# Two squared-ReLU MLPs in a fused fp32 block: wide up products, down products with tokens on partitions, two modulation groups moved

## The reference, cut to what matters

```python
mod = (sc @ w_mod[l] + b_mod[l])[:, None, :]          # 1024 x 6144 for each l
sh1, sc1, g1, sh2, sc2, g2 = jnp.split(mod, N_MOD, axis=-1)
...
u = rms_norm_2(h, norm2_g[l]) * (1.0 + sc2) + sh2     # modulate
a = jnp.maximum(u @ w_mlp1[l], 0.0)                   # 1024 -> 4096
h = h + g2 * ((a * a) @ w_mlp2[l])                    # 4096 -> 1024
```

## Time and profile before

| | |
|---|---|
| median of 3 runs | 1496.66 us (1496.38 to 1497.01) |
| the profiled execution | 1496.03 us, its span from first to last instruction 1494.2 us |
| granted TensorE clock | 1.0 over the span |
| busy: TensorE / VectorE / ScalarE / GpSimd | 98% / 82% / 55% / 8% |
| `mlp0`, from TensorE's first down to the pool stage | 1124.33 to 1290.82 us |
| `mlp1`, the same to TensorE's last matmul | 1323.24 to 1490 us |

### The profile page before, as it was taken

One profiled execution on the slowest core, in us unless ns is written; L12 is line 12 of the kernel. 1 busy time (PEld: TensorE's weight loads), 2 busy tenths in 40 slices (PEclk: granted clock), 3 DMA queues, 4 the chain that ended last, 5 costly groups with the idle time before them and its releaser, 6 DMA issues.

```text
span 1494.2 us, 26569 instructions
## 1 busy us (share of the span) xinstructions
PE 1471.7 (98%) x10462; PEld 1368.6 (92%) x10462; DVE 1226.4 (82%) x1722; ACT 820.8 (55%) x1195; POOL 116.4 (8%) x70
## 2 busy tenths in 40 slices
PE   7999999999999999999999999999999999999999
PEld 7999999999998899999779999987689999999998
DVE  7999898989988879999777988884777998885564
ACT  6554568655456645556765455554654544564442
POOL 0013100001311102111000211100001212000000
PEclk9999999999999999999999999999999999999999
DMA  7667663556675547666243776743235887346540
GB/s 271 252 242 254 239 234 130 225 187 238 238 267 197 227 168 282 236 246 250 85 141 136 287 257 250 253 156 137 106 142 203 305 289 274 141 165 222 177 170 29
DMA packets 44419, 310.43 MB, mean 208 GB/s; under 512 B 5728, under 2 KB 5984, under 8 KB 7200
## 3 DMA queue, kind: packets, MB, share of 16 engines
q1 hardware_dynamic: 42048, 303.33, 55.3%
q0 software_dynamic: 1696, 4.68, 1.1%
q10 hardware_dynamic: 576, 1.05, 0.2%
HBM read 307.93 MB, written 1.05 MB: 207 GB/s over the span
## 4 chain that ended last, share of the span: by engine, by line
PE 94%; DVE 3%; ACT 2%; issue 0%; DMA 0%; SPq 0%; DVEq 0%; ACTq 0%
PE psum L1901 18%; PE psum L1981 18%; PE psum L1907 17%; PE psum L1908 17%; PE psum L1992 9%; PE psum L2148 3%; PE psum L2154 3%; PE psum L2153 3%; DVE w_lo L1074 1%; PE psum L2466 1%; PE psum L2477 1%; PE psum L2396 0%; PE psum L2361 0%; DMA x<-x_in 0%; PE psum L2267 0%
## 5 line engine op out<-in xcount | busy, mean ns | idle before, releaser
L1074 DVE TENSOR_TENSOR w_lo<-raw,w_hi 128x1024 fp32r<-128x1024 f32 x478 | 591.0, 1252 | 78.0 <-ACT w_hi L528 77.4
L528 ACT ACTIVATE w_hi<-raw 128x1024 fp32r<-128x1024 f32 x478 | 486.1, 1047 | 66.3 <-PE psum L1901 40.4
L1901 PE MATMUL psum<-hid_hi,w_hi 128*128 128x256 f32 x1220 | 346.1, 284 | 1.1 <-DVE hid_lo L1352 1.1
L1907 PE MATMUL psum<-hid_lo,w_hi 128*128 128x256 f32 x1220 | 345.3, 283 | 0.0
L1908 PE MATMUL psum<-hid_hi,w_lo 128*128 128x256 f32 x1220 | 345.2, 283 | 0.0
L1901 PE MATMUL psum<-u,w_hi 128*128 128x256 f32 (+1 forms) x1104 | 317.3, 287 | 11.0 <-DVE u L1171 9.7
L1907 PE MATMUL psum<-u,w_hi 128*128 128x256 f32 (+1 forms) x1104 | 311.4, 282 | 0.0
L1908 PE MATMUL psum<-u,w_lo 128*128 128x256 f32 (+1 forms) x1104 | 310.9, 282 | 0.0
L1981 PE MATMUL psum<-u,w_hi 128*128 128x512 f32 x1152 | 274.8, 391 | 0.0
L1981 PEld LDWEIGHTS psum<-u,w_hi 128*128 128x128 f32 x1152 | 211.7, 188 | 41.0
L1901 PEld LDWEIGHTS psum<-hid_hi,w_hi 128*128 128x128 f32 x1220 | 233.9, 192 | 1.6 <-DVE hid_lo L1352 1.5
(11 more groups left out here) (272 smaller groups left out, 1411.3 us busy)
## 6 DMA issues: line engine op xcount, KB each, us to landing
raw<-stream SPq DMA_DIRECT2D x288, 1024.0 KB, 4.8
buf<-tab POOLq DMA_DIRECT2D x2, 768.0 KB, 5.5
x<-x_in SPq DMA_DIRECT2D x2, 512.0 KB, 7.0
buf<-ctx_in POOLq DMA_DIRECT2D x1, 1024.0 KB, 8.1
buf<-poolmat POOLq DMA_DIRECT2D x1, 1024.0 KB, 5.1
out<-x ACTq DMA_DIRECT2D x4, 256.0 KB, 2.1
buf<-late POOLq DMA_DIRECT2D x1, 640.0 KB, 4.1
mod<-mod_row POOLq DMA_DIRECT2D x28, 2.0 KB, 1.9
```

The lines of the kernel that those rows point to most:

```text
L528: sc.activation(w_hi[:, u], raw[:, u], ACT.Copy).then_inc(S.hi_ready, 1)
L1074: ve.tensor_tensor(w_lo[:, u], raw[:, u], w_hi[:, u].bitcast(F32), ALU.subtract).then_inc(S.lo_ready, 1)
L1901: ins = te.matmul(dst, w_hi[:, w], hi, start=first, stop=False, skip_group_check=True)
L1907: te.matmul(dst, w_hi[:, w], lo, start=False, stop=False, skip_group_check=True)
```

## The change

- **Ups from step 5 on** (`WIDE = 5`). VectorE makes x · gain · rstd into a spare buffer (`both_full`, 8 chunks of 256 columns), ScalarE adds the shift and rounds (`both_hi`, 8), VectorE makes the rest (`both_lo`, 8). TensorE then makes each up unit of steps 5 to 15 as 8 matmuls of 512 columns and 8 of 256. ScalarE copies the low half out of PSUM (`copy_sums`), VectorE adds the halves (`added`) and takes ReLU and square in one instruction. The shift column, the scaling and the ReLU on ScalarE go in those steps.
- **Downs 0 to 13 with tokens on partitions** (`down_tokens`): `hid` is now the stationary operand (128 x 128) and 512 columns of weights the moving one, so a unit is 12 matmuls of 512 columns in place of 24 of 256. At the end the four banks are split into hi and lo (`token_sums_hi` on ScalarE, `token_sums_lo` on VectorE, four each, during up 15). Down 14 is made in the old layout into the cleared banks, then 32 matmuls with the identity as moving operand, 128 columns each, turn the split sums round and add them (`turn_sums`), then down 15.
- **Early steps reordered.** The scaling of step 1 has a buffer of its own and comes right behind that of step 0. The `both_*` work is put between steps 1 and 3 on ScalarE and VectorE, and the pumps of this part are placed anew.
- **Modulation.** Groups 22 and 23 move from `mlp0` to `mlp1`. In `mlp0` the units per step are now 2, 1, 1 repeated over steps 3 to 14; in `mlp1` one in each of steps 4 to 11.
- `u`'s rows are 1032 columns apart (1024 before), and the MLPs' narrow operands lie at their end; in the pool stage `shift_operand(1)` on ScalarE comes behind the first block of operands.

The core of the diff, in the order constants, ScalarE, VectorE, TensorE:

```diff
-HOME = {"ffn0": range(0, 4), "ffn1": range(4, 8), "ffn2": range(8, 13), "ffn3": range(13, 18), "mlp0": range(18, 24),
-        "mlp1": range(24, 24)}
+HOME = {"ffn0": range(0, 4), "ffn1": range(4, 8), "ffn2": range(8, 13), "ffn3": range(13, 18), "mlp0": range(18, 22),
+        "mlp1": range(22, 24)}
...
-           "ffn3": [0] * 4 + [1, 1, 2, 1, 2, 1] + [1] * 12, "mlp0": [0] * 3 + [2] * 12 + [0], "mlp1": [0] * MLS}
+           "ffn3": [0] * 4 + [1, 1, 2, 1, 2, 1] + [1] * 12, "mlp0": [0] * 3 + [2, 1, 1] * 4 + [0], "mlp1": [0] * 4 + [1] * 8 + [0] * 4}
...
+WIDE = 5
+TOKENS = MLS - 2
...
+                def both_hi(k):
+                    act.wait_ge(S.both_full, NC * m + k + 1)
+                    sc.activation(m_both[:, k, 0:T], ck(buf[3])[:, k, :], ACT.Identity, bias=part(m, 3, k)).then_inc(S.both_hi, 1)
...
+                relu(0)
+                relu(1)
+                hi(0)
+                pump_to(c0 + RING - 1)
+                relu(2)
+                hi(1)
+                pump_to(c0 + 9)
+                for k in range(4):
+                    both_hi(k)
+                hi(2)
+                pump_to(c0 + 3 + RING)
+                for k in range(4, NC):
+                    both_hi(k)
+                pump_to(pumped(2))
+                for j in range(3, MLS):
+                    (relu if j < WIDE else copy_sums)(j)
+                    if j < MLS - 2:
+                        pump_one(pumped(j))
+                    hi(j)
+                    if j == MLS - 2:
+                        for b in range(4):
+                            token_sums_hi(b)
+                    pump_to(pumped(j))
...
+                scaled(0, t2, "s", 4)
+                scaled(1, t_one, "s_one", 6)
+                squared(0)
+                pump_to(c0 + AHEAD)
+                low(0)
+                scaled(2, third, "s_third", 2)
+                pump_to(c0 + RING - 1)
+                squared(1)
+                pump_to(c0 + RING)
+                low(1)
+                pump_to(c0 + 9)
+                for k in range(4):
+                    both_full(k)
+                squared(2)
+                pump_to(c0 + 2 + RING)
+                low(2)
+                pump_to(c0 + 3 + RING)
+                for k in range(4, NC):
+                    both_full(k)
+                for k in range(4):
+                    both_lo(k)
+                pump_to(pumped(2))
+                for j in range(3, MLS):
+                    if j < WIDE:
+                        scaled(j, t2, "s", 4 + 2 * (j % 2))
+                    else:
+                        added(j)
...
+                    low(j)
+                    if j == 3:
+                        for k in range(4, NC):
+                            both_lo(k)
+                    if j == MLS - 2:
+                        for b in range(4):
+                            token_sums_lo(b)
+                    pump_to(pumped(j))
...
+                    if j >= WIDE:
+                        if j == WIDE:
+                            pe.wait_ge(S.both_lo, NC * (m + 1))
+                        wide_hi(c, 0, bank, m_both).then_inc(S.unit_used, 1)
+                        wide_hi(c + 1, 0, bank + 1, m_both)
+                        wide_lo(c, 0, bank, 0, m_both)
+                        began, done = wide_lo(c + 1, 0, bank + 1, 0, m_both)
+                        began.then_inc(S.unit_used, 1)
+                        done.then_inc(S.up_ready, 1)
+                        begun[0] = c + 1
...
+                def token_products(c, n, par, b, first, last, begins):
+                    tt, w = b // 2, slice((c % RING) * UNIT + (b % 2) * 512, (c % RING) * UNIT + (b % 2 + 1) * 512)
+                    t = slice(n * T + tt * P, n * T + (tt + 1) * P)
+                    ins = te.matmul(psum[:, b, :], hid_hi[:, par, t], w_hi[:, w], start=first, stop=False, skip_group_check=True)
+                    if begins:
+                        ins.then_inc(S.unit_used, 1)
+                    te.matmul(psum[:, b, :], hid_lo[:, par, t], w_hi[:, w], start=False, stop=False, skip_group_check=True)
+                    return te.matmul(psum[:, b, :], hid_hi[:, par, t], w_lo[:, w], start=False, stop=last, skip_group_check=True)
+
...
+                def turn_sums():
+
+                    pe.wait_ge(S.ident_ready, 1)
+                    for half in (sum_hi, sum_lo):
+                        for n in range(NC):
+                            for tt in range(2):
+                                te.matmul(bank2(n // 2)[:, n % 2, tt * P:(tt + 1) * P],
+                                          half[:, 2 * tt + n // 4, (n % 4) * P:(n % 4 + 1) * P], ident_r[:, :], start=False, stop=False,
+                                          skip_group_check=True)
 
...
-                down(0, first=True)
-                down(1)
-                for j in range(3, MLS):
+                down_tokens(0)
+                down_tokens(1)
+                for j in range(3, MLS - 1):
                     up_pair(j)
-                    down(j - 1)
+                    down_tokens(j - 1)
+                up_pair(MLS - 1)
+                down(TOKENS, first=True)
+                turn_sums()
                 down(MLS - 1, last=True)
 
```

More of the change, by code:

```diff
@@ L200, in __init__ @@
         self.up_copied = sem("up_copied")
+        self.both_full = sem("both_full")
+        self.both_hi = sem("both_hi")
+        self.both_lo = sem("both_lo")
+        self.ident_ready = sem("ident_ready")
+        self.tok_sums = sem("tok_sums")
+        self.sums_hi = sem("sums_hi")
+        self.sums_lo = sem("sums_lo")
         self.up_added = sem("up_added")
@@ L509, in _ @@
                     sum_squares(n)
+            sum_groups("mlp1")
         @block.scalar
@@ new lines, in low, with both_full, both_lo @@
+                def low(j):
+                    dve.wait_ge(S.hid_hi_ready, h0 + j + 1)
+                    ve.tensor_tensor(hid_lo[:, j % 2, :], h32, hid_hif[:, j % 2, :], ALU.subtract).then_inc(S.hid_ready, 1)
+                v = ck(buf[3])
+                def both_full(k):
+                    ve.scalar_tensor_tensor(v[:, k, :], x[:, k, :], ty(gain, k), rstd[:, :], ALU.mult, ALU.mult).then_inc(S.both_full, 1)
+                def both_lo(k):
+                    dve.wait_ge(S.both_hi, NC * m + k + 1)
+                    ve.scalar_tensor_tensor(m_both[:, k, T:2 * T], v[:, k, :], part(m, 3, k), m_bothf[:, k, 0:T], ALU.add, ALU.subtract)\
+                      .then_inc(S.both_lo, 1)
@@ L1790, in _ @@
             sqrelu("mlp0")
-            modulation_in(HOME["mlp0"][3])
+            modulation_in(HOME["mlp0"][-1])
             add_bias(1, 24, 40)
@@ L1855, in _ @@
             sqrelu("mlp1")
-            modulation_in(HOME["mlp0"][-1])
+            modulation_in(HOME["mlp1"][-1])
             add_bias(1, 40, 48)
@@ L1980, in wide_hi @@
                 for k in range(NC):
-                    ins = te.matmul(bank2(bank), w_hi[:, at + k * P:at + (k + 1) * P], u_both[:, k, :], start=k == 0, stop=False,
+                    ins = te.matmul(bank2(bank), w_hi[:, at + k * P:at + (k + 1) * P], both[:, k, :], start=k == 0, stop=False,
                                     skip_group_check=True)
@@ L1991, in wide_lo @@
                 for k in range(NC):
-                    ins = te.matmul(bank2(bank)[:, 1, :], w_lo[:, at + k * P:at + (k + 1) * P], u_hi[:, k, 0:T], start=False,
+                    ins = te.matmul(bank2(bank)[:, at_half, :], w_lo[:, at + k * P:at + (k + 1) * P], hi[:, k, 0:T], start=False,
                                     stop=k == NC - 1, skip_group_check=True)
@@ new lines, in down_tokens @@
+                def down_tokens(j):
+                    c, par = unit_at(name, "down", j), j % 2
+                    pe.wait_ge(S.hid_ready, h0 + j + 1)
+                    if j < TOKENS - 1:
+                        for n in range(2):
+                            unit_ready(c + n)
+                            for b in range(4):
+                                if j == 0 and n == 0:
+                                    third_read(b)
+                                ins = token_products(c + n, n, par, b, j == 0 and n == 0, False, b == 0)
+                        if j == 0:
+                            ins.then_inc(S.first_down, 1)
+                    else:
+                        unit_ready(c + 1)
+                        for b in range(4):
+                            token_products(c, 0, par, b, False, False, b == 0)
+                            token_products(c + 1, 1, par, b, False, True, b == 3).then_inc(S.tok_sums, 1)
+                    begun[0] = c + 1
```

132 lines of the change are left out of this document (71 added, 61 removed).

## The result

The kernel after takes **1514.92 us** (median of 4 runs, 1513.73 to 1516.48), the kernel before in turn with it 1496.52 us (1496.09 to 1497.01): a ratio of 1.0124 with the interval 1.0112 to 1.0136, slower by 18.4 us. The forecast was 1500.4 us with a range to 1506.5. The direction was right; the size was wrong by more than four times, and the time lies outside the range.

The account below looks back on a forecast made before the run. TensorE, busy 98%, was taken as the bound, VectorE second. On 1496.03 us: -10.2 gain + 7.2 turning - 1.3 old stall + (0.5 + 3.3 + 0.6 + 1.5) + 2.4 waits = +4.0, 1500.0; forecast 1500.4, range 1493.0 to 1506.5.

Parts of the forecast that it names:

- The wait at down 2 of `mlp0`: TensorE waits from 17.1 to 20.4 us after down 0 for unit 14, queued behind modulation units 12 and 13: 3.3 us.
- Up 3: In `mlp0`, unit 10 is ready at 11.3 us where TensorE wants it at 10.95: 0.4 to 0.5 us lost.
- Down 4: In `mlp0`, `hid` of step 4 comes at 43.1 us against 42.5 wanted: 0.6 us, plus 1.5 for GpSimd's sum.
- GpSimd's sum: Group 18's sum in `mlp0` holds VectorE up just before units 24 and 25: 1.5 us (0 to 1.7) added.
- The laid-out queue of VectorE: Early steps of both MLPs, laid out from traced durations; rival that `mlp0`'s queue holds: about 1495 us, chance 0.20.
- The turning: 2 x 32 matmuls of 128 columns that turn the token sums, 113 ns each: +7.2 us (4.3 to 7.7).
- a short or a long one: Turning of the sums shorter or longer than the 7.2 us taken: chance 0.12 each; short together with the queue holding 0.11.
- The split sums: Four PSUM copies on ScalarE and four VectorE subtractions, covered by up 15: nothing, at most about 3 us if uncovered.
- the operands moved inside `u` ...: 0.1 us at most: Operands moved inside `u`, and `shift_operand(1)` put behind one block: 0.1 us at most.
- The rival on spacing: Wide forms space differently with `hid` stationary or rows 1032 apart: 5 ns a matmul, 3.4 us over 672, either direction; no separate chance.
- "2.4 us" of waits in `mlp1`: Waits of 0.7 (down 1), 0.6 (up 3), 0.4 (down 2), 0.7 us (down 3), in place of today's 1.3.
- the gain of 10.2 us: Both MLPs' wider matmuls: 22 ups x 0.11 = 2.4 us and 28 downs x 0.28 = 7.8 us won.

Follow-up runs that it names:

- the run with ScalarE ahead: Kernel after with one edit: in `mlp1` ScalarE makes its unit splits one unit ahead of VectorE's, as in `mlp0`; 1509.70 us.
- the repairs: In the kernel after: `u`'s rows 1056 apart (alone 1504.95 us), and modulation from step 5 of `mlp0` with ScalarE one unit ahead in `mlp1` (alone 1504.32); together 1495.42.
- both edits of the queues: Kernel after with `mlp0`'s modulation units from step 5 instead of 3, and ScalarE one unit ahead in `mlp1`; 1504.32 us with rows left at 1032.

## Why the prediction was wrong, step by step

**Right.** The wait at down 2 of `mlp0`: 3.3 us laid out, 2.9 in the row and 3.1 by the starts. Up 3: 0.4 to 0.5 laid out, 0.4 by the starts. Down 4: 0.6 and 1.5 for GpSimd's sum, 2.05 in the row. That sum did what the earlier trace rows said; the timelines of after, GpSimd and VectorE, show two `w_lo` in 4.41 us beside it where 2.36 is usual:

```profile
1165.57 4.13 POOL L482 PARTITION_ALL_REDUCE mod_row<-buf  x1 [73.06 <-DVE buf L1130]
...
1165.39 4.41 DVE L1121 TENSOR_TENSOR w_lo<-raw,w_hi 128x1024 fp32r<-128x1024 f32 x2
```

The laid-out queue of VectorE is to be seen, too: four `both_lo`, the two modulation units, and only then four `w_lo`, on the first of which down 2 waits:

```profile
1143.61 1.67 DVE L1411 SCALAR_TENSOR_TENSOR u<-buf,mod,u 128x256 fp32r<-128x256 f32 x4
1145.19 0.48 DVE L1129 TENSOR_SCALAR buf<-raw,tiny 128x512 f32<-128x512 f32 x1
1145.71 2.40 DVE L1130 SCALAR_TENSOR_TENSOR buf<-raw,tiny,buf 128x512 f32<-128x512 f32 x3
1148.02 4.62 DVE L1121 TENSOR_TENSOR w_lo<-raw,w_hi 128x1024 fp32r<-128x1024 f32 x4
```

The turning: 7.2 us forecast, 64 x 110 ns = 7.1 measured. That is within 2 ns of the weight loads' 112 in the earlier trace rows and fits the reading that weight loads space it, though no run varied the load. No run shows a turning of the 4.3 us at which the range given for it begins, nor a short or a long one, to which chances were given: in after each 32 starts take 3.53 us, 110 ns a matmul. Of the waits laid out in `mlp1`, 0.7 at down 1 and 0.6 at up 3 came, at about 0.7 each by the starts. The split sums cost nothing, and VectorE's busy share went from 88 to 78% in `mlp0` and from 59 to 67% in `mlp1`.

**Wrong, 1: the sentence "the operands moved inside `u` ...: 0.1 us at most".** Those 0.1 us were in truth about 8: 8.8 in the kernel before with the rows' distance changed, 10.0 in after when it goes to 1056, where 1056 by itself is 1.4 better than 1024. The argument priced the term by the instructions, none of which changed. The rival on spacing had the right price, 5 ns on a matmul, but counted it over the 672 token products of the MLPs alone. `u` is an operand far beyond the MLPs: 1152 matmuls of 512 columns in the FFNs and the 576 of the kind of the earlier trace rows read it.

**Wrong, 2: "2.4 us" of waits in `mlp1`.** Down 4 wanted 3.0 us and was laid out at nothing, while down 2 and down 3 waited less than laid out (0.4 each by the starts, 0.4 and 0.7 laid out); in all 5.1 us for 2.4. I had stopped laying out queues at down 3 and said that from step 5 on the chain had 1.7 us of margin with "the two unit splits put between"; down 4 lay in neither part. That margin took `w_hi` as ready when VectorE comes to `w_lo`. In `mlp1` it was not, twice, by 3.6 us in all. That ScalarE runs ahead by one unit in `mlp0` only was in the code, in one `int(...)` of the bound.

**Wrong, 3: half clock.** No row of before has the clock under 1.0 in the MLPs, and the sum had no term for it. In after it fell to 0.5 twice for about 3.4 us: down 4 of `mlp0` lost 1.65 us and down 4 of `mlp1` 1.40 (6.98 for 5.58). The larger of the two, 1.65 us, is what after gives as a bound for each wait of 2.1 to 2.9 us.

**Wrong, 4: the gain of 10.2 us.** A token down takes 5.58 us instead of 5.48, in both layouts of `u` that were tried, and 5.44 once `hid`, its stationary operand, lies in front: 28 x 0.1 = 2.8 us less gain. (That a wide up takes 5.65 instead of 5.56 in after belongs to the first point; with rows 1056 apart it takes 5.55.) The gain by kind also stood on a thin base: 28 downs at 0.28 us against a turning of 7.2 left 0.6 us, so the token products could hardly win even as forecast.

**The account**, in the profiled execution: layout 4.6 + 0.4 ahead of the MLPs and between them, 22 x 0.09 = 2.0 in the wide ups and 4 x 0.1 in the narrow ups 3 and 4, together 7.4; token downs 2.8; waits in `mlp1` 5.1 for 2.4, +2.7; waits in `mlp0` 5.8 for 5.9, -0.1; clock 1.65 + 1.40; the tail behind the last matmul 0.4; the turning and the last two downs shorter than taken, -0.5. Together 15.8 us, to be held against 19.5 - 4.0 = 15.5; the 0.3 us between them are not assigned.

**What stays open.** Why the distance of rows and the place of a tile shift a matmul's spacing: the runs give the numbers and exclude the chip (the kernel before, beside each of these kernels on its chip, stays between 1496.2 and 1496.5) and the instructions, of which only the addresses differ; they do not show the mechanism. Nor is it shown why the clock fell behind the 2.1 us wait at down 4 in after and not behind the 2.9 us one before it, while in the run with ScalarE ahead it fell behind that one. Of the four executions of after two have a mean granted clock of 0.998, the profiled one among them, and two of 0.996, so the number of such stretches probably differs between executions, and the account above is of one. The last 1.1 us between the sum of the repairs and both together is not assigned.

## What to carry to other kernels

A change of a tile's size or row length is an edit to every instruction that reads it: a price per matmul is worth its whole count in the program. It is to be measured alone, in the kernel before, ahead of judging what it came with. When a unit of work is put into a chain between two engines as filler, both halves of it must be ahead of the chain on *both* engines; a filler whose first half stands behind the chain's next link is no filler. And a wait of 2 to 3 us on TensorE is to be priced with the clock behind it, 1.4 to 1.7 us more for each stretch here.

## What the runs showed of the hardware

- A rounded-fp32 matmul of 512 columns came every 228 to 234 ns and one of 256 every 118 to 120 ns by the moving operand's place and the distance of its rows (table above); with `hid` as stationary operand, 227 or 232 ns by where `hid` lies. Over a kernel of 10,000 matmuls this moved the time from 1493.8 to 1505.1 us with nothing altered but addresses.
- Rounded-fp32 matmuls of 128 columns with a new stationary operand each came every 110 ns in after (32 starts in 3.53 us); that the load of the stationary operand is what spaces them is not shown by itself.
- The granted clock went to 0.5 for some 3.4 us around a wait of 2.1 to 2.9 us in three of the kernels (after, rows 1056 apart in after, ScalarE ahead) and once behind a gap of 1.8 us (rows 1040 apart), and not in the MLPs of the ones with both edits of the queues, where no wait reached 1 us. Other gaps of this length had no such stretch: 2.9 us at down 2 in after, 1.7 us in the kernel before.
- Beside a sum over the partitions on GpSimd two `w_lo` of VectorE took 4.41 us in after, where two take 2.36: 2.05 us more together.
